# The up products of two MLPs as seven products of quarters, with the sums of weight quarters made in DRAM

## The reference

```python
def rms_norm(x, g):
    xf = x.astype(jnp.float32)
    y = xf * lax.rsqrt(jnp.mean(xf * xf, axis=-1, keepdims=True) + EPS)
    return (y * g.astype(jnp.float32)).astype(x.dtype)

def sq_relu_mlp(h, w_up, w_down):              # w_up 1024 x 4096, w_down 4096 x 1024
    return jnp.square(jax.nn.relu(h @ w_up)) @ w_down

x = x + mix
x = x + sq_relu_mlp(rms_norm(x, norm_mlp_g[layer]), mlp_w_up[layer], mlp_w_down[layer])
```

## Time and profile before

| | |
|---|---|
| median of three runs | 1812.29 us (1812.17 to 1812.43) |
| profiled execution | 1811.19 us |
| its span, first to last instruction | 1809.5 us |
| TensorE busy in the span | 1794.8 us, 99% |
| VectorE, ScalarE, GpSimd busy | 70%, 45%, 16% |
| one slab | up stage 44 us, down stage 38 us |

### The profile page before, as it was taken

One profiled execution on the slowest core, in us unless ns is written; L12 is line 12 of the kernel. 1 busy time (PEld: TensorE's weight loads), 2 busy tenths in 40 slices (PEclk: granted clock), 3 DMA queues, 4 the chain that ended last, 5 costly groups with the idle time before them and its releaser, 6 DMA issues.

```text
span 1809.5 us, 21889 instructions
## 1 busy us (share of the span) xinstructions
PE 1794.8 (99%) x8580; PEld 1455.8 (80%) x8580; DVE 1270.9 (70%) x1680; ACT 808.7 (45%) x1064; POOL 288.0 (16%) x237
## 2 busy tenths in 40 slices
PE   9999999999999999999999999999999999999998
PEld 7888888888877668888888878788887888888886
DVE  7896858686879865767686887666446455846757
ACT  6753534343534863444343454566323343323334
POOL 0004000000145864000000031111001321011012
PEclk9999999999999999999999999999999999999999
DMA  6233253443234003452524222122332223431612
GB/s 234 94 117 116 71 186 90 127 133 94 65 99 148 16 2 116 139 163 47 186 56 154 65 85 84 56 70 71 98 112 82 94 93 140 140 117 47 175 59 76
DMA packets 152053, 186.25 MB, mean 103 GB/s; under 512 B 7472, under 2 KB 120240, under 8 KB 151952
## 3 DMA queue, kind: packets, MB, share of 16 engines
q1 hardware_dynamic: 143712, 165.93, 28.1%
q0 software_dynamic: 7696, 18.41, 4.9%
q10 hardware_dynamic: 544, 0.52, 0.1%
HBM read 182.58 MB, written 2.14 MB: 102 GB/s over the span
## 4 chain that ended last, share of the span: by engine, by line
PE 87%; DVE 8%; ACT 2%; issue 1%; POOL 1%; DMA 0%; SPq 0%; DVEq 0%; ACTq 0%; POOLq 0%
PE bank L998 27%; PE bank L1000 26%; PE bank L999 26%; PE bank L1034 1%; PE bank L1219 1%; DVE work L2460 1%; PE bank L1245 1%; DVE t L2457 1%; DVE wlo L2058 1%; DVE XC L2155 1%; PE bank L1354 1%; PE bank L1372 1%; ACT whi L1481 1%; DVE sq_e L2566 1%; PE bank L1223 1%
## 5 line engine op out<-in xcount | busy, mean ns | idle before, releaser
L998 PE MATMUL bank<-Ahi,whi 128*128 128x512 f32 x1400 | 550.2, 393 | 1.4 <-DVE wlo L2084 1.1
L1000 PE MATMUL bank<-Ahi,wlo 128*128 128x512 f32 x1400 | 545.1, 389 | 0.0
L999 PE MATMUL bank<-Alo,whi 128*128 128x512 f32 x1400 | 544.9, 389 | 0.0
L2058 DVE TENSOR_TENSOR wlo<-stage,whi 128x2048 fp32r<-128x2048 f32 (+1 forms) x133 | 304.8, 2292 | 175.2 <-ACT whi L1481 175.1
L1481 ACT ACTIVATE whi<-stage 128x2048 fp32r<-128x2048 f32 (+1 forms) x139 | 262.7, 1890 | 218.8 <-PE bank L1000 192.6
L998 PEld LDWEIGHTS bank<-Ahi,whi 128*128 128x128 f32 x1400 | 262.2, 187 | 64.7 <-issue 7.9
L1000 PEld LDWEIGHTS bank<-Ahi,wlo 128*128 128x128 f32 x1400 | 262.2, 187 | 55.9
L999 PEld LDWEIGHTS bank<-Alo,whi 128*128 128x128 f32 x1400 | 262.3, 187 | 55.5 <-issue 1.2
L998 PE MATMUL bank<-whi,Hh 128*128 128x512 f32 x602 | 234.8, 390 | 0.0
L999 PE MATMUL bank<-wlo,Hh 128*128 128x512 f32 x602 | 234.3, 389 | 0.0
L1000 PE MATMUL bank<-whi,Hl 128*128 128x512 f32 x602 | 234.2, 389 | 0.0
(11 more groups left out here) (356 smaller groups left out, 2468.1 us busy)
## 6 DMA issues: line engine op xcount, KB each, us to landing
stage<-in_mlp_w_up SPq DMA_DIRECT2D x32, 1024.0 KB, 5.4
stage<-in_w_in SPq DMA_DIRECT2D x22, 1024.0 KB, 5.1
stage<-in_w_ffn_in SPq DMA_DIRECT2D x22, 1024.0 KB, 4.9
quad<-in_mlp_w_down SPq DMA_DIRECT2D x16, 1024.0 KB, 6.8
stage<-in_mlp_w_down SPq DMA_DIRECT2D x16, 1024.0 KB, 4.8
quad<-in_mlp_w_down POOLq DMA_DIRECT2D x8, 1024.0 KB, 8.6
stage<-in_rec_w_in SPq DMA_DIRECT2D x6, 1024.0 KB, 5.3
stage<-in_att_w_in SPq DMA_DIRECT2D x6, 1024.0 KB, 5.1
```

What stands on the lines that cost most here:

```text
L998: e.matmul(ps, hi, rh, start=first, stop=False, skip_group_check=onto)
L999: e.matmul(ps, hi, rl, start=False, stop=False, skip_group_check=onto)
L1000: return e.matmul(ps, lo, rh, start=False, stop=last, skip_group_check=onto)
L2058: e.tensor_tensor(lo_of(u)[:, 0:nk, 0:n], source(u), f32(hi_of(u)[:, 0:nk, 0:n]), ALU.subtract).then_inc(s_lo[slot_of[u]], 1)
```

## The change

- **Up stage.** `strassen_up` in place of `gemm`. The weights of a slab (1024 features by 1024 hidden) are four quarters of 512 x 512, and the normalized `X` too (512 features by 256 tokens). Seven products (`UP`: W11, S2, S3, S1, W12, S4, W22), each 48 matmuls whose moving operand has 256 columns, in place of 192 matmuls of 512. S1 to S4 are sums of weight quarters. Partial sums stay in PSUM: banks 6 and 7 collect W11, S2, S1, S4, and ScalarE copies them out between products (`up_copy`); VectorE adds these copies to other banks (`up_add`), and ScalarE takes the maximum with 0 and squares (`squared`).
- **Sums in DRAM.** `build` makes S1 to S4 by eight DMAs of the GpSimd queue, DRAM to DRAM: four copies and four that add. Each waits for the one before to land. For MLP 0 a DMA moves 1 MB and they go slab by slab; for MLP 1 there are eight of 4 MB, issued from the third slab of MLP 0 on and between the steps of the attention. They are put between GpSimd's other work by `make(n)`.
- **Right operands.** T1 to T4 of the normalized `X` are made by VectorE and ScalarE at the head of each MLP (`right_of`, `fill_right`, `right_hi`, `right_lo`). Their memory takes the place of `X`, which eight DMAs store in DRAM (`kept`) and two bring back in the last slab.
- **Root.** The root of the norm is no longer a factor in `relu`; `1/(mean + eps)` per token (`rsq`) is a factor of each down product, in `add_sum` and in ScalarE's copies.
- **Down weights.** T1 and T4 are made by DMAs of the GpSimd queue that add in place (`first_quarter`, `last_quarter`), T2 still by VectorE.

```diff
+        def first_quarter(key):
+            e.wait_ge(*split_done((*key, "B11")))
+            e.dma_start(quadrant(key, "q11"), slabs[key]["q12"], accum_op=ALU.add).then_inc(s_acc, 16)
+        def last_quarter(key):
+            e.wait_ge(*split_done((*key, "T2")))
+            e.dma_start(quadrant(key, "q11"), slabs[key]["q21"], accum_op=ALU.add).then_inc(s_acc, 16)
...
+            built_before()
+            e.dma_start(made("S1"), quarter(1, 1)).then_inc(s_build, 16)
+            yield
+            built_before()
+            e.dma_start(made("S1"), quarter(1, 0), accum_op=ALU.add).then_inc(s_build, 16)
...
+        def mlp_quarters(l, g, *steps):
+            first_quarter(("dn", l, g))
+            add_quarter(("dn", l, g))
+            make(steps[0])
+            last_quarter(("dn", l, g))
+            make(steps[1])
```

```diff
+            take_unit(("up", l, g, "W12"))
+            for x in range(2):
+                half("W12", x, begin(("ua", l, g, x)), False).then_inc(*ring.put(("ua", l, g, x)))
+            take_unit(("up", l, g, "S4"))
+            for x in range(2):
+                e.wait_ge(*up_read(l, g, "S1", x))
+                half("S4", x, banks[6 + x], True).then_inc(s_mid, 1)
+                if x == 0:
+                    take_unit(("up", l, g, "W22"))
+                e.wait_ge(*up_added(l, g, "W22", x))
+                half("W22", x, ring.bank(("ud", l, g, x)), True).then_inc(*ring.put(("ud", l, g, x)))
```

`half` is 24 matmuls: half x of the hidden features of a product, blocks 2x and 2x + 1. In the down stage, block i of the left operand now belongs to half x = i // 2:

```diff
+                if key[0] == "dn":
+                    m, x = slab_no[key], i // 2
+                    return (s_slo, 2 * m + x + 1) if r == 2 else (s_hlo, 4 * m + 2 * x + r + 1)
```

VectorE's program at the end of a slab's up stage, with the new functions it calls:

```diff
+        def first_of_up(l, g, x):
+            n, part = 4 * l + g, slice(2 * x, 2 * x + 2)
+            w = HwA[:, part, :, :]
+            e.wait_ge(s_q, 8 * n + UP_SQUARED.index(("W12", x)) + 1)
+            e.tensor_tensor(w[:, :, 3, :], w[:, :, 0, :], w[:, :, 4, :], ALU.subtract).then_inc(s_sum, 1)
...
+            e.tensor_tensor(HlA[:, part, 0, :], w[:, :, 0, :], f32(HhA[:, part, 0, :]), ALU.subtract).then_inc(s_hlo, 1)
...
+                lo(u0 + 7)
+                first_of_up(l, g, 0)
+                up_add(l, g, "W21", 0)
+                second_of_up(l, g, 0)
+                first_of_up(l, g, 1)
+                up_add(l, g, "W21", 1)
+                lo(u0 + 8)
+                second_of_up(l, g, 1)
+                up_low_sums(4 * l + g, 0)
```

More of the change, by code:

```diff
@@ L18 @@
 TURN = [4, 5, 6, 7, 0, 1, 2, 3]
+UP = ["W11", "S2", "S3", "S1", "W12", "S4", "W22"]
+UP_RIGHT = {"W11": "B11", "S2": "T2", "S3": "T3", "S1": "T1", "W12": "B21", "S4": "B22", "W22": "T4"}
+UP_DONE = ["W11", "S2", "S3", "S1", "S4"]
+UP_READ = ["W11", "S2", "S1", "S4"]
+UP_SQUARED = [("W22", 0), ("W22", 1), ("W11", 0), ("W11", 1), ("W12", 0), ("W21", 0), ("W12", 1), ("W21", 1)]
+SUMS = ["S1", "S3", "S2", "S4"]
 class Ring:
@@ L85, in product_order, with program @@
     return out + [("e", m) for m in todo]
-def program(nc, I, out, scratch):
+def program(nc, I, out, scratch, sums, kept):
     ctx = ExitStack()
@@ L384, in ring_mlp @@
         for g in range(4):
-            blocks(("up", l, g), 8, [("root", l)] if g == 0 else ())
+            ring.add(("ud", l, g, 0), ("ud", l, g, 1))
+            if g == 0:
+                ring.add(("root", l))
+            ring.add(("ua", l, g, 0), ("ua", l, g, 1))
             ring_slab(("dn", l, g))
@@ new lines, in steps_of, with make @@
+        def steps_of(*parts):
+            for part in parts:
+                yield from part
+        making = steps_of(build(0, [0]), build(0, [1]), build(0, [2]), build(0, [3]), build(1, [0, 1, 2, 3]))
+        def make(n):
+            for _ in range(n):
+                next(making)
+        def mlp_quarters(l, g, *steps):
[4 more added lines that the diff above has]
+            make(steps[1])
@@ L835, in gpsimd_program @@
         keep(maskb[:, 0:64], ALU.is_ge, -1, 0, 63).then_inc(s_const, 1)
+        e.wait_ge(*ring.full(("xr", 3)))
+        make(14)
         for m in range(8):
             square("mlp0", m, ring.free(("ro", m)))
-        e.wait_ge(*ring.free(("root", 0)))
-        for g in range(4):
-            add_quarter(("dn", 0, g))
+        make(5)
+        mlp_quarters(0, 0, 2, 4)
+        mlp_quarters(0, 1, 2, 4)
+        mlp_quarters(0, 2, 1, 1)
+        mlp_quarters(0, 3, 1, 1)
         for i in range(7):
@@ L1040, in root, with token_sums @@
             e.matmul(ps[:, :], ones[:, :], (sqa_e if fill == "att" else sqa)[:, :], start=True, stop=True).then_inc(*ring.put(label))
+        def token_sums(l):
+            ps = begin(("root", l))
+            e.wait_ge(s_sq, SQ_END[f"mlp{l}"])
+            for j in range(4):
+                t = e.matmul(ps[:, j:j + 1], sq_mlp[1][l][:, j * 128:(j + 1) * 128], onesc[:, :], start=True, stop=True)
+            t.then_inc(*ring.put(("root", l)))
         e.wait_ge(s_const, CONST["ident"])
@@ new lines, in vector_program, with up_add @@
+        fill_right(0, "ro")
+        def up_add(l, g, which, x):
+            t = UT[which][x]
+            if which == "W11":
+                label = ("ua", l, g, x)
+                e.wait_ge(*up_read(l, g, "W11", x))
+                e.wait_ge(*ring.full(label))
+            elif which == "W22":
+                label = ("ud", l, g, x)
+                e.wait_ge(*up_read(l, g, "S1", x))
+                e.wait_ge(*up_done(l, g, "S3", x))
+            else:
+                label = ("ud", l, g, x)
+                e.wait_ge(*up_read(l, g, "S2", x))
+                e.wait_ge(*ring.full(label))
+            ps = ring.bank(label)[:, :].rearrange("p (a t) -> p a t", a=2)
+            done = (s_up_added, 1) if which == "W22" else ring.take(label)
+            e.tensor_tensor(t[:, :, :], ps, t[:, :, :], ALU.add if which == "W11" else ALU.subtract).then_inc(*done)
@@ new lines, in mlp @@
+                lo(u0 + 4)
+                if g == 0:
+                    right_lo(l, "T4", 11)
+                lo(u0 + 5)
+                if g == 0:
+                    label = ("root", l)
+                    e.wait_ge(*ring.full(label))
+                    e.tensor_scalar(rsq[:, 0:4], ring.bank(label)[:, 0:4], 1.0 / 1024, 1e-6, ALU.mult, ALU.add).then_inc(*ring.take(label))
+                    e.wait_ge(*ring.free(label))
+                    e.reciprocal(rsq[:, 0:4], rsq[:, 0:4]).then_inc(*st.inc())
+                    e.wait_ge(*st.now())
+                    e.tensor_scalar(rsq[:, 4:8], rsq[:, 0:4], -1.0, None, ALU.mult).then_inc(s_rstd, 1)
+                    e.wait_ge(s_rstd, RSTD[f"mlp{l}"])
```

548 lines of the change are left out of this document (405 added, 143 removed).

## The result

The changed kernel takes **1968.78 us** (median of 4 runs, 1964.56 to 1976.63), the kernel before 1812.23 us (1810.66 to 1812.43): a ratio of 1.0871, 95% interval 1.0836 to 1.0906. Forecast were 1849 us and a range of 1806 to 1876: the sign is right, the size is a quarter of what came (37 us forecast, 156 measured), and the range is missed by 93 us.

A forecast was written before the change was run, and what follows sets the result against it. TensorE, busy 99% of the span, was taken as the bound. 1809.5 - 25.6 + 48.6 + 6 + 8 = 1846.5 us of span, 1849 us with time outside it; range for 8 in 10: 1806 to 1876.

The forecast's parts named there:

- up stages: Up stages: 2688 matmuls of 256 columns replace 1536 of 512, a gain of 25.6 us, 3.2 a slab.
- end-of-up chain, with T4: End of up stage: late operands make TensorE wait 6.1 us a slab, 48.6 us lost; T4 itself in time.
- right operands at the heads: Head of each MLP: making T1 to T4 of X costs nothing while under TensorE's stream.
- building DMAs beside loads: MLP 0, slabs 0 to 2: building DMAs slow the stage loads, 2 us a slab, 6 us; ends 0 and 25.
- kk: Attention: the keys' copy queues behind a 4 MB adding DMA at 4.8 us a MB; 8 us lost.
- hand timeline: Up stage's end, written out per engine from its start: T2's split ends at 62.7 us, wanted at 60.3.
- I take 2 us a slab, 6 us: MLP 0 loads: a stage buffer's round takes 13.1 us against TensorE's 11.5, most of the excess absorbed by the splits' lead.
- split by 75.5, wanted 79.0: Down stage: T4's quarter, asked for at 62.7 us and landing 8.6 us later, is split before TensorE wants it.
- the DMA engines become the bound in MLP 0: Rival, MLP 0: late squares, T4's or T1's quarter and loads add 20 to 50 us, giving 1870 to 1900; chance 0.15.
- Cost nothing as far as they lie under TensorE's stream: X's stores and reloads, the right operands (11 us of VectorE's work per MLP head) and rsq add no time.
- the case without that cover: Head of each MLP: right operands not hidden under TensorE's stream would cost 2 to 5 us an MLP.
- The signs: Down stages: about 6 us of waits naming VectorE's lines, eight times; about 8 us waiting for a DMA before kk's products.

The follow-up runs named there:

- no_builds: Changed kernel without any building DMA, the units S1 to S4 loaded from plain quarters of the up weights: 1883.56 us (1.0398).
- experiment 3: Changed kernel, two runs: the adding DMA for T4's quarter left out, 1924.56 us; T3's adds put ahead of the next stage's first split on VectorE, 1947.73 us.
- experiment 6: Changed kernel with the attention's first 4 MB adding DMA issued behind the copy of the keys instead of ahead of w_uv: 1964.89 us (1.0844).
- head_order: Changed kernel with ScalarE's copies of W11's banks, in each MLP's first slab, ahead of the third unit's split and T3's and T1's high parts: 1962.32 us.
- no_builds_reordered: no_builds plus T3's adds earlier, VectorE making the squares, head_order's edit and a later VectorE split at the second MLP's end: 1855.47 us (1.0243).
- no_builds_ends: no_builds with the second unit's split at MLP ends behind three fills of the norm's operand on ScalarE, in MLP 1 four on VectorE: 1871.55 us.

## Why the prediction was wrong, and where it held

Per part, forecast against measured (us of span; the measured ones add up to 153.5, of 153.8 between 1809.5 and 1963.3):

| part | forecast | measured | read from |
|---|---|---|---|
| up stages | -25.6 | -25.6 | 8 x (43.5 - 40.3) |
| end-of-up chain, with T4 | 48.6 | 61.3 | down stages of `no_builds`, the last of each MLP at the mean of the others |
| right operands at the heads | 0 | 20.4 | first up stages of `no_builds` |
| ends of the MLPs | not in the sum | 16.5 | turns of `no_builds` |
| building DMAs beside loads | 6 | 59.5 | head and MLP 0, with and without builds |
| `kk` | 8 | 21.4 | attention, with and without builds |

**The gain** is right to 0.1 us. The Trainium skill's rule (TensorE: Matmul & The Clock Gate, "Wait — 56ns, not 53.3ns?") would have given 38.8 as an estimate (the prediction's own figures for it add up to that, and not to 38.6). The rows of the changed kernel have 0.120 us a start at 256 columns, where that rule has 0.109, so for these matmuls the measurement decides against the Trainium skill.

**The chain** is right as a mechanism, and the hand timeline is within 0.4 us. (Its waits, as listed, add up to 6.2 a slab, and 8 x 6.1 is 48.8; that moves nothing.) The waits of the kinds that it forecast, 48.6 in all, measured 34.1 in `no_builds`, 4.3 a slab: 1.6 for B11's block 2 (forecast 2.1), 0.5 for T1's (0.8), 2.1 for T2 (2.4), none for B21's and for T1's split. T4's, which it had at nothing, are another 6.3. What was mis-sized is what follows a wait: 21 us in which TensorE's starts are further apart than 0.227. A wait was priced at its own length, and costs half as much again. So 48.6 is near 61.3 in part because an excess in one place met a term left out in another.

**The step that failed most** is "I take 2 us a slab, 6 us". The work was sized well: 80 to 93 us of DMA work in each of slabs 0 to 2 of MLP 0 was forecast, and 0.85 x 101.5 = 86 measured. Then a load "of 5.4 us beside a building step takes about 8.5"; the median is 8.6, but the ones that decided, ahead of T4 in slabs 1 and 2, took 15 and 16. And T4 was said to be "split by 75.5, wanted 79.0", which holds in slabs 1 and 2 (the split was 2.4 us early in slab 1) and not in 0 and 3 (2.8 and 1.9 us late), while T4's product waits for a second thing, the adds of T3's product, and those stand behind the late load (in slab 0 behind T4's late split). The slack that I counted was that of the split, not of everything the product waits for (experiment 3). Turning that order round won 17.9 us in MLP 0, where the building costs 56.9. The rest wasn't taken apart by a run: the trace has it as longer waits at other places in the same slabs, with the clock down behind many of them. MLP 0 has 81 us of waits and 26 us of slower starts over its 319 of work. The rival "the DMA engines become the bound in MLP 0" was the nearest, with 0.15 and 20 to 50 us; it deserved a larger chance once its own sum said 80 to 93 of 84. But its 1900 us too are 69 short.

**`kk`.** The order of things was forecast and came: the copy waits behind the 4 MB. The size was the adding price, 4.8 us a MB, from a queue in which half was not adding: the 4 MB were to take 20 us and took some 31. With 6 us a MB the text itself had 13, and 15.5 were measured; the other 6 of the attention's 21.4 were in no term. The rule cited with it (the Trainium skill, DMA: Bandwidth & Descriptors, "Queues, rings and completion order") is stated there for the queues that SyncE and ScalarE issue to, and it adds that a later descriptor may finish its write before an earlier one, so "can't overtake" is more than it says; the row agrees in the order: `kk` landed only when the 4 MB had. What no step had is that GpSimd's own instructions wait for building steps too (experiment 6).

**"Cost nothing as far as they lie under TensorE's stream"** failed for the right operands. VectorE's room was counted; ScalarE's program wasn't read: W11's copies, without which S2's product can't start, stand behind T2's, T3's and T1's high parts. `head_order` confirms it by moving them (5.0 us in MLP 1). It is about half of the term: in `no_builds_reordered` the first up stages are 4.4 and 4.7 us shorter than in `no_builds`, of 11.3 and 9.1; what the rest goes back to stays open. Likewise the end of the MLP: which product frees the slot of a later unit was not followed, and `no_builds_ends` confirms that it costs 12.4 of the 16.5. And the sum left out its own sentence for the case without that cover, 2 to 5 us an MLP; 11.3 and 9.1 came.

**The signs** that the prediction named wouldn't have caught this. Its waits are there, VectorE's lines are the ones named, the loads slowed down as it said, and `kk` waits for a DMA. But a wait that names VectorE doesn't tell that VectorE itself stood behind a late load.

Only argued, not shown: that the slower starts come from the waits ahead of them, since no run changes the clock by itself, and which late load or step each of the other waits in MLP 0 goes back to.

## What to carry to other kernels

When a change adds an operand, write down for the product that uses it everything that it waits for, its bank's last reader included, and then what stands ahead of each of these on its engine: a late load costs TensorE wherever one in-order engine has it ahead of something urgent. Judge added DMA traffic by that and not by its share alone: at 0.78 of the DMA engines' time the building steps cost the old kernel nothing in two slabs, and the same steps cost the new one, at 0.83, 19.5 us in them. And where the engines' work by your own sum comes as near to the stretch as here (80 to 93 of 84), give the bound case a large chance.
